# Gate and branch products between the small matmuls of gated linear attention, another staging slot in layer two, and one low part ahead of a rotation

## The reference, cut to what matters

```python
# gated linear attention, chunks of 16 tokens, 4 heads of 64
o = einsum('bhtd,bhde->bhte', q_dec, state) + einsum('bhts,bhse->bhte', attn, vc)
state = exp(bL)[..., None] * state + einsum('bhsd,bhse->bhde', k_dec, vc)
# gates and branches of the first block
gates = sigmoid(p["gate"] + merge_gate_b).reshape(B, S, 4, D)
merged = gates[:, :, 0] * y_ml + gates[:, :, 1] * y_gla + gates[:, :, 2] * y_conf + gates[:, :, 3] * y_sc
# the second block: rotations in front of the indexer and of attention
q = rope_partial(q); k = rope_partial(k); iq = rope_partial(iq); ik = rope_partial(ik)
# its feed-forward part, the last work before the output
return (silu(a) * b) @ w_down
```

## Time and profile before

| what | value |
|---|---|
| runs shown | 1598.61, 1603.83, 1605.95 us |
| median | 1603.83 us |
| profiled execution | 1597.15 us |
| its span, first to last instruction | 1595.3 us |
| TensorE, matmuls | 1567.4 us busy, 98% of the span |
| VectorE / ScalarE / GpSimd | 1102.7 / 679.0 / 246.5 us busy |
| mean granted TensorE clock | 0.993 of full speed |

### The profile page before, as it was taken

The page is one execution under the profiler, slowest core; times in us unless marked ns, Lnnn a source line. Parts: engine busy times, 40 slices in busy tenths (PEclk is TensorE's granted clock), DMA queues, the critical chain, the costliest instruction groups (busy, mean ns, idle before and its releaser), DMA issues.

```text
span 1595.3 us, 20449 instructions
## 1 busy us (share of the span) xinstructions
PE 1567.4 (98%) x7760; PEld 1290.0 (81%) x7760; DVE 1102.7 (69%) x1523; ACT 679.0 (43%) x898; POOL 246.5 (15%) x143
## 2 busy tenths in 40 slices
PE   6999999999999999999999999999999999999997
PEld 5888788788888888888888987777888888888886
DVE  5569554448787677745887777777355788967884
ACT  5343453233234633323556622354533433333564
POOL 2110033110002033233100001420123111111000
PEclk9999999999999999999999999999999999999999
DMA  9132123117552288832553343212123578623552
GB/s 375 56 116 96 54 79 104 56 53 276 199 211 80 75 295 285 291 109 85 202 188 120 108 143 99 76 63 80 54 79 106 175 279 295 226 91 105 211 178 92
DMA packets 71246, 233.88 MB, mean 147 GB/s; under 512 B 11175, under 2 KB 15876, under 8 KB 65284
## 3 DMA queue, kind: packets, MB, share of 16 engines
q1 hardware_dynamic: 67584, 213.48, 38.7%
q10 hardware_dynamic: 2612, 16.89, 2.7%
q0 software_dynamic: 976, 2.51, 0.5%
HBM read 205.91 MB, written 25.17 MB: 145 GB/s over the span
## 4 chain that ended last, share of the span: by engine, by line
PE 92%; DVE 3%; ACT 2%; DMA 1%; issue 1%; SPq 0%; ACTq 0%; DVEq 0%
PE bank L1641 22%; PE bank L1643 21%; PE bank L1642 21%; PE bank L2129 4%; PE bank L2130 3%; PE bank L2131 3%; PE bank L1656 2%; PE bank L1658 2%; PE bank L1657 2%; PE bank L1743 1%; PE bank L2312 1%; PE bank L1649 1%; PE bank L1651 1%; PE bank L1650 1%; PE bank L1986 1%; DVE w_lo L2940 1%
## 5 line engine op out<-in xcount | busy, mean ns | idle before, releaser
L1641 PE MATMUL bank<-h_hi,w_hi 128*128 128x512 f32 (+2 forms) x1424 | 554.5, 389 | 1.5 <-DVE w_lo L2369 1.5
L1643 PE MATMUL bank<-h_hi,w_lo 128*128 128x512 f32 (+2 forms) x1424 | 546.4, 384 | 0.0
L1642 PE MATMUL bank<-h_lo,w_hi 128*128 128x512 f32 (+2 forms) x1424 | 545.9, 383 | 0.0
L1641 PEld LDWEIGHTS bank<-h_hi,w_hi 128*128 128x128 f32 x1424 | 267.7, 188 | 68.8 <-issue 15.7
L1643 PEld LDWEIGHTS bank<-h_hi,w_lo 128*128 128x128 f32 x1424 | 267.7, 188 | 52.7
L1642 PEld LDWEIGHTS bank<-h_lo,w_hi 128*128 128x128 f32 x1424 | 267.9, 188 | 50.9 <-issue 1.0
L957 ACT ACTIVATE w_hi<-w_raw 128x2048 fp32r<-128x2048 f32 x107 | 204.6, 1912 | 168.9 <-PE bank L1643 114.8
L2369 DVE TENSOR_TENSOR w_lo<-w_raw,w_hi 128x2048 fp32r<-128x2048 f32 x90 | 205.8, 2286 | 41.3 <-ACT w_hi L957 40.3
L891 POOL TENSOR_TENSOR work<-work 128x512 f32 x44 | 95.7, 2175 | 396.6 <-ACT work L1389 396.6
L854 POOL TENSOR_TENSOR w_lo<-w_raw,w_hi 128x2048 fp32r<-128x2048 f32 x17 | 79.3, 4666 | 481.4 <-ACT w_hi L957 481.4
L2129 PE MATMUL bank<-w_hi,h_hi 128*128 128x512 f32 x252 | 98.8, 392 | 0.6 <-DVE w_lo L2940 0.5
(11 more groups left out here) (346 smaller groups left out, 2288.9 us busy)
## 6 DMA issues: line engine op xcount, KB each, us to landing
w_raw<-in_w_in_units SPq DMA_DIRECT2D x94, 512.0 KB, 4.6
w_raw<-in_ffn_w_up_units SPq DMA_DIRECT2D x44, 512.0 KB, 4.6
down_sums<-work SPq DMA_DIRECT2D x22, 1024.0 KB, 4.9
w_raw<-in_w_up_units SPq DMA_DIRECT2D x44, 512.0 KB, 5.0
work<-in_ada_w_units ACTq DMA_DIRECT2D x16, 1024.0 KB, 6.5
work<-in_ffn_w_down SPq DMA_DIRECT2D x27, 512.0 KB, 5.9
work<-in_w_down SPq DMA_DIRECT2D x27, 512.0 KB, 5.9
w_raw<-down_sums SPq DMA_DIRECT2D x14, 768.0 KB, 4.9
```

The lines of the kernel that those rows point to most:

```text
L1641: pe.matmul(dst, w_hi[s][:, at:at + n], hi, start=first, stop=False, skip_group_check=onto)
L1642: pe.matmul(dst, w_hi[s][:, at:at + n], lo, start=False, stop=False, skip_group_check=onto)
L1643: return pe.matmul(dst, w_lo[s][:, at:at + n], hi, start=False, stop=last, skip_group_check=onto)
```

## The change

Three edits. In layer two, unit 18 of the down projection is loaded into the slot that the rule gives it (the one of unit 14) and waits for the low part of unit 14. Between the small matmuls of `gla_before`, after every fifth chunk, one triple of wide matmuls is put, six for each c: for c = 0 the last two triples of gate2 tile 4 and the first four of tile 5, for c = 1 the last two of gate2 tile 7 and the four of y2 tiles 0 and 1. What is left of tile 5 follows `gla_states(5)`, and y2 goes on with tile 2; the sum of squares of c = 1 now stands behind y2 tile 3. In VectorE's stream `lo(U["q"] + 1)` moves ahead of `rotate("ik")`.

```diff
-        SLOT = {n: [(g if g < 2 else 3 if g == THIRD + 1 else (g - 2) % 4) ^ first % 2 for g in range(DOWN_UNITS)] for n, first in DOWN.items()}
+        SLOT = {n: [(g if g < 2 else 3 if (n, g) == ("1", THIRD + 1) else (g - 2) % 4) ^ first % 2 for g in range(DOWN_UNITS)] for n, first in DOWN.items()}
...
-        GATE2_AFTER = {0: 0, 1: 1, 2: 2, 3: 3, 5: 5, 6: 6}
+        GATE2_AFTER = {0: 0, 1: 1, 2: 2, 3: 3, 6: 6}
...
-                        v = u - 1 if g == THIRD + 1 else u - 2 if g < 4 else u - 4
+                        v = u - 1 if (n, g) == ("1", THIRD + 1) else u - 2 if g < 4 else u - 4
...
                 if n in GATE2_AFTER:
                     column_tile("gate2", GATE2_AFTER[n])
+                elif n == 5:
+                    column_part("gate2", 5, 4, KT)
...
-            def gla_before(c):
+            def gla_before(c, product):
...
+                    if k % 5 == 0:
+                        product(k // 5 - 1)
                 return mm
+
+            def branch_part(n, k):
+
+                t = T["y2"][n]
+                if k == 0:
+                    wait_free(pe, t)
+                mm = three(bank[t.bank][:, :], U["y2"], k * D + n * P, P, y_hi[:, 2 + k, :], y_lo[:, 2 + k, :], k == 0, k == 1)
+                if k:
+                    done(mm, t)
+
+            def between(i):
+
+                column_part("gate2", *((4, 6 + i, 7 + i) if i < 2 else (5, i - 2, i - 1)))
+
+            def between_last(i):
+
+                if i < 2:
+                    column_part("gate2", 7, 6 + i, 7 + i)
+                    return
+                if i == 2:
+                    pe.wait_ge(sem("y_lo"), 4)
+                    weights_ready(U["y2"])
+                branch_part((i - 2) // 2, i % 2)
...
-                column_part("gate2", tile, 4, KT)
+                column_part("gate2", tile, 4, 6)
                 gla_within(2 * c + 1)
-                done(gla_before(c), T["gl_o"][c])
+                done(gla_before(c, between_last if c else between), T["gl_o"][c])
...
-            branch_unit("y2", 2, 4, lambda n: gla_mean_square(1) if n == 1 else None)
+            column_unit(U["y2"], T["y2"][2:], 2, y_hi[:, 2:4, :], y_lo[:, 2:4, :], at=2, behind=lambda n: gla_mean_square(1) if n == 1 else None)
...
             rotate("iq")
+            lo(U["q"] + 1)
             rotate("ik")
-            lo(U["q"] + 1)
```

## The result

| kernel | median, us | runs | lowest to highest |
|---|---|---|---|
| before | 1598.57 | 20 | 1597.64 to 1605.95 |
| after | 1605.77 | 20 | 1599.78 to 1614.34 |

The ratio is 1.0033, 95% interval 1.002 to 1.0045: some 5 us slower, within the half per cent but clear of no change (the ratio is an estimate from all runs; the two medians alone lie 7.2 us apart). I had expected 2.5 us less. The profiled execution of after took 1601.08 us; its span of 1599.3 is 4.0 us more than the one of before. It is among the shortest of its kernel: the 20 spans run from 1598.0 us at a mean granted clock of 0.994 to 1612.5 us at 0.982. The median clock is 0.988; in the 35 runs of the kernel before beside the first experiments it is 0.991.

A forecast was written before the change was run, and what follows sets the result against it. TensorE bound the kernel, its matmuls covering 98% of the span. Part A +1.0, part B -2.8 and part C -0.7 summed to -2.5 us: 1601.3 us against a median of 1603.83, range 1596 to 1607.

The forecast's parts named there:

- I take it that it holds: Mixed stretches of small and wide matmuls, c = 0 and 1: clock stays full, -4.15 us, ends 0 and 4.15.
- part A: Wide triples between the small matmuls: clock -4.15, kind changes +3.6, wait in y2 +1.5, together +1.0 us.
- rival 2: Both mixed stretches: clock falls all the same, moved triples +8.4 us, whole sum +4.9, 1608.7 us; chance 0.1.
- changing kind: TensorE's steps from small matmuls to a wide triple and back: 0.3 us per triple, twelve make +3.6 us.
- rival 1: Weight loads slide under the wides, 1.2 us in all, and no wait in y2: sum -6.5, 1597.4 us; chance 0.2.
- the new wait in y2: TensorE at y2 tile 6 waits about 1.5 us for VectorE to read tile 2; ends 0 and 2.
- part B: Last down projection, layer two: unit 18's earlier load brings the chain to unit 19 sooner, -2.8 us.
- Part C: Low part ahead of rotate("ik"): TensorE's 0.71 us wait before q tile 2 goes, -0.7 us.
- rival 3: Slot and low part give their time back before unit 19 and the next score matmul: sum about 0, 1604 us; chance 0.15.
- The base: Forecast sum was set on 1603.83 us, the median of the runs shown, 6.7 us above the profiled execution of 1597.15.

The follow-up runs named there:

- e5: Kernel before with only the triples put between the small matmuls, slot and low part as before: 1607.35 us, ratio 1.0042.
- e7: Changed kernel, but VectorE's norm of c = 1 stands behind y2 tile 3 instead of tile 1: 1604.91 us, ratio 1.0039 to before.
- e1: Kernel before with unit 18's slot and the low part ahead of the rotation, no product moved: 1595.59 us, ratio 0.9981.
- e8: Changed kernel with 8 and 10 triples in three blocks per c, and norm, squares and ScalarE's split reordered: 1593.82 us, ratio 0.9968 to before.
- e9: e8 with its 8 and 10 triples dealt out singly, one after every third chunk: 1597.91 us, ratio 0.9987 to before.
- e6: Kernel before with the slot of unit 18 alone: 1597.50 us, ratio 0.9983.
- e11: Kernel before with unit 18's slot, the early low part and e8's orders of norm and split, no product moved: 1595.95 us, ratio 0.9983.
- e4: Changed kernel, but for c = 0 a triple after every third chunk, ten in all: 1601.43 us, ratio 1.0015 to before.

## Why the prediction was wrong, step by step

- **The step that failed: "I take it that it holds".** I priced the clock at -4.15 us. Between the marks the profiles give +0.4 us for it in after, +4.3 in e5 and, since 7.7 - 3.7, +4.0 in e7. The times agree: after and e1 differ by part A: 1.0033 / 0.9981 is 8.3 us. Borders 12 x 0.31 = 3.7 and the wait of 1.46 leave about +3 for the clock, with an uncertainty of about 3 us; e5 against the kernel before leaves +1.5. So the term was off by 5 to 8 us, and a gain did not come at all. The time at half clock says the same. The profiles of the four kernels without part A have 14.0 us at half clock in the two stretches, each of them; e5 and e7 have 28.0. The profiled after has 14.0 as well, but the median clock of its runs, 0.988 against 0.991, is 0.003 x 2 x 1600 = some 10 us more at half clock, of which the mean doesn't say where they fall. With the mixtures held (e8, e9) there is none in the two stretches, and then the clock's term is about -3.7 us: its size was right, its condition was not.
- **Why the row did not carry it.** I leaned on one window at the start of the kernel, from 37 to 38 us, where the other matmuls were narrow, not small. The clock didn't stay up there: it fell 4 us into the first run of those narrow matmuls (from 28.74 us on), stood at half until 36 us (the row below, of the kernel before), and was back less than 1 us before my window. That row stands in the same trace, and I passed it over. Nearer still is my own: 7 us of small matmuls bring the clock down, and two thirds of each round of the mixture were still small matmuls and borders.

```profile
33.00:34.00 1.00, 1.00 (x6) 1.00 (x6) 0.32 (x2) 0.00 (x0) 0.00 (x0) 0.50 1.07 434
```

- **My rival 2 is what happened**, with a chance of 0.1: I called "wides fill only about a third of the mixture" an argument for it and gave it too little. Its price of +4.9 us is near the measured ratio (+5.3), but partly by luck: it leaves out the wait in y2, 1.5 us, without a reason, and with it part A would be +9.9 (e5's profile has +9.5, that of after +5.6). Its account was partly off too: in the profiled after the fall of c = 1 came only 11.7 us behind its first small matmul; in e5 and e7 both stretches were down for 14 us.
- **Right: changing kind.** 0.3 us per triple forecast, 0.31 read. The Trainium skill, "TensorE: Matmul & The Clock Gate", section "Step-by-step: what each phase is for", lets the next weight load slide under the running matmul; at these borders the trace disagrees by those 0.31 us a triple, so the prediction's rival 1 is out.
- **Right: the new wait in y2** (1.5 forecast, 1.46 read, 1.47 in e5), for the reason given: split, low part, factor, norm, tile 2. One link was off: the low part was done at 360.49, and the factor ended last; I had the low part last.
- **Right: part B.** -2.8 forecast, -2.75 in the profile, 0.9983 for it alone (2.7 us, interval 0.8 to 4.8). **Part C:** its wait went as forecast (0.81 in e6, none in e1), but the two ratios, 0.9983 and 0.9981, can't tell 0.7 us. The prediction's rival 3 is out by e1. One thing I passed over in the earlier trace rows: in the kernel before unit 18 took 6.11 us from its first matmul to that of unit 19, where 18 wides at 0.23 are 4.1, because the clock fell behind the wait of 2.16 us (0.50 from 1580 to 1582 us). It cost nothing, since unit 19's low part was done only at 1584.11; it is why TensorE alone would have given 4.3.
- **The base.** I set the sum on the 1603.83 us of three runs; the median of 20 is 1598.57. The profiled execution, 1597.15, was the usual one, and two of the three runs were long. That 1605.77 lies inside my range of 1596 to 1607 us is luck: on the right base the range would have been 1591 to 1602. I also took 8 us for the least that a measurement of this kernel can tell; the interval of its ratio turned out to be 2 us to either side.

## What to carry to other kernels

Wide matmuls between small ones paid here only where they were enough and in few places: six single triples per stretch lost 8 us with their borders and a wait, eight to ten in three blocks gained about 2, and the same as singles kept the clock but paid 3 to 4 us in borders. Before a mixture is trusted to keep the clock, look at which mixture of the same matmuls did so in a trace, not at another mixture that happens to stand at 1.00, and read the windows on both sides of the one that pleases. And a tile moved ahead on TensorE asks for its bank sooner: the order of its reader has to move with it.

## What the runs showed of the hardware that was not expected

- A fall is not over when wide matmuls are there again. In c = 0 of after the clock was down for 10 us, and triples stood among the small matmuls for the first 7 of them; in e5 and e7 it lasted 14 us in each stretch. The Trainium skill, "TensorE: Matmul & The Clock Gate", section "HAM oscillation — how this bites in real kernels", ties the loss of the clock to idle gaps between bursts. In the window of e5 at 350 us TensorE was busy for 10.00 of 10 us at a clock of 0.50, so here the trace disagrees. One fall does stand behind a gap, the one in unit 18 of the kernel before, after 2.16 us of idle time.
- Small 64 x 64 matmuls of 16 columns cost the same at both clocks: 1.28 us for 20 records at full, 1.29 at half.
- The larger part of the spread lies outside the change. e1 and e11 have the same half-clock time from 300 to 370 us, but their profiled spans are 1598.5 and 1592.1 us, and 6.2 of these 6.4 us are there before the first `gla_states` (276.13 against 269.89). The window at the start tells them apart (e1 first, then e11, then after). In all thirteen profiles the clock is at half somewhere between 30 and 40 us, where the narrow matmuls are; in the kernel before it is back at 36 us, in after at 39, in e1 at 46, and there it falls once more. That makes 3.6, 6.6 and 16.8 us at half clock, and after's 1.8 us of delay in front of the change. What decides when it comes back is open. e4, e5, e7 and e9 have one more fall, between 174 and 179 us, also in front of the change. So a mean clock alone doesn't tell where it was lost.

```profile
26.00:56.00 30.00, 28.67 (x149) 25.79 (x148) 17.34 (x28) 14.26 (x22) 0.57 (x1) 0.72 0.56 223
```

```profile
26.00:56.00 30.00, 28.84 (x177) 25.60 (x177) 19.66 (x30) 15.81 (x24) 0.57 (x1) 0.94 0.66 259
```

```profile
26.00:56.00 30.00, 28.71 (x170) 25.84 (x170) 19.51 (x30) 15.66 (x24) 0.57 (x1) 0.89 0.64 249
```
